# Delta rule of a two-block transformer kernel: from six units of full 128x128 blocks to three groups of compact 64x64 blocks, with the scan's steps placed between the levels of the next group's inverse

## What is computed

```python
diff = gc[..., :, None] - gc[..., None, :]            # gc: cumulated gates inside the chunk
decay = jnp.where(lower, jnp.exp(jnp.where(lower, diff, 0.0)), 0.0)
a_mat = jnp.where(strict, jnp.einsum('nbhid,nbhjd->nbhij', kb, kc) * decay, 0.0)
t_inv = lax.linalg.triangular_solve(eye + a_mat, eye, ...)   # inverse of a 64x64 unit triangle
u_val = t_inv @ vb
w_key = t_inv @ (kb * exp(gc))
attn_intra = jnp.where(lower, (qc @ kc.T) * decay, 0.0)
def step(s, xs):                                     # one chunk after the other
    v_new = u_i - w_i @ s
    o_i = qd_i @ s + a_i @ v_new
    s = s * jnp.exp(gl_i) + kd_i.T @ v_new
```

## Time and profile before

| | us |
|---|---|
| median of 3 runs (3429.64 to 3438.17) | 3431.32 |
| the profiled execution's own time | 3429.59 |
| its span | 3427.8 |
| PE busy (share of the span) | 3205.1 (94%) |
| DVE busy | 1474.0 (43%) |
| POOL busy | 1566.4 (46%) |
| ACT busy | 739.4 (22%) |
| DMA, mean over the span | 139 GB/s |

### The profile page before, as it was taken

The page is one execution under the profiler, slowest core; times in us unless marked ns, Lnnn a source line. Parts: engine busy times, 40 slices in busy tenths (PEclk is TensorE's granted clock), DMA queues, the critical chain, the costliest instruction groups (busy, mean ns, idle before and its releaser), DMA issues.

```text
span 3427.8 us, 39498 instructions
## 1 busy us (share of the span) xinstructions
PE 3205.1 (94%) x15738; PEld 2494.3 (73%) x15738; DVE 1474.0 (43%) x2741; ACT 739.4 (22%) x1544; POOL 1566.4 (46%) x1104
## 2 busy tenths in 40 slices
PE   6999999989999999999998999979998989879998
PEld 4767778767778776777877777766557888558876
DVE  2664433435550266444244555212204555267721
ACT  3333331111110233333111111001122111121110
POOL 5444555565546543445556455530003324156654
PEclk9999999999999999999999999979989999989999
DMA  5444444446666443444444666531100000135554
GB/s 185 145 133 138 152 149 165 149 151 229 229 226 196 160 148 123 148 142 144 163 154 147 210 243 229 178 136 44 61 25 1 1 1 1 37 112 191 195 181 144
DMA packets 129239, 477.03 MB, mean 139 GB/s; under 512 B 14352, under 2 KB 14352, under 8 KB 128160
## 3 DMA queue, kind: packets, MB, share of 16 engines
q1 hardware_dynamic: 70592, 261.23, 24.2%
q0 software_dynamic: 57024, 207.64, 16.8%
q10 hardware_dynamic: 1440, 5.64, 0.4%
HBM read 472.32 MB, written 2.13 MB: 138 GB/s over the span
## 4 chain that ended last, share of the span: by engine, by line
PE 79%; DVE 9%; issue 5%; POOL 4%; ACT 1%; DMA 1%; POOLq 0%; DVEq 0%; ACTq 0%
PE dense L673 18%; PE dense L675 17%; PE dense L674 17%; PE dense L756 7%; POOL raw_lo L2179 2%; PE scores L866 2%; PE O L900 1%; PE turned L1108 1%; PE scores L1117 1%; PE turned L888 1%; POOL squares_sum L2198 1%; PE scores L673 1%; PE scores L674 1%; PE scores L675 1%; PE O L934 1%
## 5 line engine op out<-in xcount | busy, mean ns | idle before, releaser
L2179 POOL TENSOR_TENSOR raw_lo<-raw,weights_hi 128x1024 fp32r<-128x1024 f32 x396 | 951.9, 2404 | 75.7 <-DMA raw<-stream 40.4
L673 PE MATMUL dense<-h_hi,weights_hi 128*128 128x512 f32 x2208 | 890.9, 403 | 31.8 <-POOL raw_lo L2179 16.3
L675 PE MATMUL dense<-h_hi,raw_lo 128*128 128x512 f32 x2208 | 867.6, 393 | 0.0
L674 PE MATMUL dense<-h_lo,weights_hi 128*128 128x512 f32 x2208 | 867.3, 393 | 0.0
L2172 POOL DMA_DIRECT2D weights_hi<-stream x396 | 228.9, 578 | 1090.4 <-PE dense L675 972.7
L673 PEld LDWEIGHTS dense<-h_hi,weights_hi 128*128 128x128 f32 x2208 | 419.4, 190 | 160.5 <-issue 68.1
L675 PEld LDWEIGHTS dense<-h_hi,raw_lo 128*128 128x128 f32 x2208 | 418.6, 190 | 91.2
L674 PEld LDWEIGHTS dense<-h_lo,weights_hi 128*128 128x128 f32 x2208 | 419.8, 190 | 80.9
L673 PE MATMUL dense<-hidden_hi,weights_hi 128*128 128x512 f32 x528 | 207.6, 393 | 10.9 <-POOL raw_lo L2179 6.3
L674 PE MATMUL dense<-hidden_lo,weights_hi 128*128 128x512 f32 x528 | 206.4, 391 | 0.0
L675 PE MATMUL dense<-hidden_hi,raw_lo 128*128 128x512 f32 x528 | 206.4, 391 | 0.0
(11 more groups left out here) (326 smaller groups left out, 4713.6 us busy)
## 6 DMA issues: line engine op xcount, KB each, us to landing
raw<-stream SPq DMA_DIRECT2D x473, 512.0 KB, 3.6
weights_hi<-stream POOLq DMA_DIRECT2D x396, 512.0 KB, 4.7
decays<-stream ACTq DMA_DIRECT2D x8, 512.0 KB, 4.3
gates<-f_scratch SPq DMA_DIRECT2D x2, 1536.0 KB, 9.7
x<-x_in SPq DMA_DIRECT2D x2, 1024.0 KB, 8.5
dft<-dft SPq DMA_DIRECT2D x4, 512.0 KB, 7.0
out<-x SPq DMA_DIRECT2D x4, 512.0 KB, 2.7
const<-consts SPq DMA_DIRECT2D x1, 1088.0 KB, 4.9
```

Source lines behind the costliest of these rows:

```text
L673: nc.tensor.matmul(banks[b], wh, xh, start=first, stop=False)
L674: nc.tensor.matmul(banks[b], wh, xl, start=False, stop=False)
L675: return nc.tensor.matmul(banks[b], wl, xh, start=False, stop=final)
L2179: nc.gpsimd.tensor_tensor(raw_lo(n % RAW_SLOTS), raw(n % RAW_SLOTS), w_hi(w % HI_SLOTS), ALU.subtract).then_inc(weights_lo, 1)
```

## The change

Every matrix of the stage is now compact: 128 x 512 holds 8 blocks of 64x64 per direction and partition half, that is two token blocks (j = 0, 1) times four heads side by side, and the two chunks of a token block one above the other (partitions 0 to 63 and 64 to 127). Two token blocks make a group; there are three groups of two blocks in place of six units.

- The decays of all three groups and both directions are made ahead of the k transposes: POOL multiplies the gates by a triangle (`rowsum`, 6 tiles), DVE makes `rowbar` (6 tiles), PE sums them by 12 products of 512 columns in the two dense banks, and ACT takes 6 exponentials.
- Key-key and query-key products are made once per group for both directions, as 64x64x64 products; A and X are then scaled by DVE with two instructions each, in place of 4 per head.
- Products of the inverse are 64x64x64 and use the tile corners (rows and columns 0 to 63, or 64 to 127, of the array) in turn. Only the update of TT is multiplied; T comes from TT by a DVE transpose (STREAM_TRANSPOSE) of 32x32 blocks, which is the whole transpose since up to level 4 all blocks are at most 32 wide. The update is written over Z in the same bank (`turned`).
- In place of scaled keys and values, POOL scales TT for w (`tt_gain`) and DVE scales TT for u (`tt_beta`).
- The four scan steps of group g - 1 stand between the levels 1 to 4 of group g: the read between Z and the update, the write behind the update. The last four steps stand alone. DVE decays the state ahead of the level's subtracts, and adds behind them; the output through the state is scaled by ACT, four instructions a direction (`output_state`).
- The third DMA of constants is smaller (1472 columns for 2176), and tiles of the stage lie at other places.

The new code of the stage, cut to its core (the removed functions `unit` and `scan` are shown above; the diff's DVE functions `make_a`, `make_x` and `level_zero`, ACT's part, the products for the outputs and the tables of places are left out; one `level_z` and one `level_update` of PE do both directions):

```diff
-UNITS = 6
+UNITS, GROUPS, STEPS = 6, 3, 12
 FIRST_L = 2
+PAIR_GDN = tuple([o[2 * g] // 2 for g in range(GROUPS)] for o in ORDER_GDN)
+LATENT_PAIRS = [(d, PAIR_GDN[d][g]) for g in (1, 2) for d in range(2)]
...
+                    nc.tensor.matmul(dense[:, k % 2, :], chunk_ones, rowsum[k], start=True, stop=False)
+                    nc.tensor.matmul(dense[:, k % 2, :], ident, rowbar[k], start=False, stop=True
+                                     ).then_inc(row_ready, 1)
...
+            def level_z(g, lev):
+                for d in range(2):
+                    pe.wait_ge(t_masked, level_no(g, lev, d))
+                    pe.wait_ge(t_ready_g, level_no(g, lev - 1, d))
+                    if lev == 1 and g:
+                        pe.wait_ge(u_copied, 4 * g)
...
+                                last = nc.tensor.matmul(turned[hs, d, c64(j, h)], a_level[d][hs, c64(j, h)],
+                                                        tt_mat[d][hs, c64(j, h)], start=True, stop=True)
+                    last.then_inc(t_z, 1)
+            def level_update(g, lev):
+                for d in range(2):
+                    pe.wait_ge(t_zc, turn_no(g, lev, d))
+                    for j in range(2):
                         for h in range(GH):
+                            for c in range(2):
+                                hs = half_rows(c)
+                                last = nc.tensor.matmul(turned[hs, d, c64(j, h)], t_mat[d][hs, c64(j, h)],
+                                                        z_mat[d][hs, c64(j, h)], start=True, stop=True)
+                    last.then_inc(t_upd, 1)
...
+                                last = nc.tensor.matmul((turned, scores)[c][:, d, c64(j, h)],
+                                                        ktok[half_rows(c), 2 * p + j, h * P:(h + 1) * P],
+                                                        tt_gain[d][half_rows(c), c64(j, h)], start=True, stop=True)
+                    last.then_inc(w_ready, 1)
...
+                        if j:
+                            pe.wait_ge(w_copied, 2 * g + d + 1)
                         for h in range(GH):
+                            for c in range(2):
+                                hs = half_rows(c)
+                                last = nc.tensor.matmul((dense, turned)[j][hs, d, h * P:(h + 1) * P],
+                                                        tt_beta[d][hs, c64(j, h)],
+                                                        vtok[hs, 2 * p + j, h * P:(h + 1) * P], start=True, stop=True)
+                        last.then_inc(u_ready, 1)
+            def scan_read(s):
+                n, i = s // 2, s % 2
+                pe.wait_ge(w_copied, 2 * (n // 2) + 2)
+                pe.wait_ge(u_copied, 4 * (n // 2) + 4)
+                if s:
+                    pe.wait_ge(c_s, 2 * s)
+                else:
+                    pe.wait_ge(ab_step, 14)
+                if latent_no(s) > 0:
+                    pe.wait_ge(c_o2, 2 * latent_no(s))
+                for h in range(GH):
+                    hc = slice(h * P, (h + 1) * P)
+                    for d in range(2):
+                        c, hs = chunk_of(d, i)
+                        last = nc.tensor.matmul(dense[hs, d, hc], wT[2 * d + c][:, c64(ORDER_GDN[d][n] % 2, h)],
+                                                state[d][:, hc], start=True, stop=True)
+                last.then_inc(c_ws, 1)
...
+            def scan_write(s):
+                n, i = s // 2, s % 2
+                pe.wait_ge(c_v, 2 * s + 2)
+                if s < STEPS - 1:
+                    pe.wait_ge(kd_ready, 2 * n + 2)
+                    for h in range(GH):
+                        hc = slice(h * P, (h + 1) * P)
+                        for d in range(2):
+                            c, hs = chunk_of(d, i)
+                            u = u_rows[2 * d + ORDER_GDN[d][n] % 2]
+                            last = nc.tensor.matmul((O[:], misc[:])[d][:, hc], kd[2 * d + n % 2][hs, hc], u[hs, hc],
+                                                    start=True, stop=True)
+                    last.then_inc(c_sd, 1)
...
+            for g in range(GROUPS):
+                for lev in range(1, LEVELS):
+                    level_z(g, lev)
+                    if g and lev < LEVELS - 1:
+                        scan_read(4 * (g - 1) + lev - 1)
+                    level_update(g, lev)
+                    if g and lev < LEVELS - 1:
+                        scan_write(4 * (g - 1) + lev - 1)
+                    if g == 0 and lev >= LEVELS - 2:
+                        turn_x(2 * (lev - LEVELS + 2))
+                        turn_x(2 * (lev - LEVELS + 2) + 1)
+                w_and_u(g)
+            for s in range(STEPS - 4, STEPS):
+                scan_read(s)
+                scan_write(s)
...
+            def level_done(g, lev):
+                for d in range(2):
+                    dve.wait_ge(t_upd, turn_no(g, lev, d))
+                    nc.vector.tensor_tensor(tt_mat[d], tt_mat[d], turned[:, d, :], ALU.subtract).then_inc(t_subbed, 1)
+                    if lev < LEVELS - 1:
+                        dve.wait_ge(t_subbed, level_no(g, lev, d))
+                        nc.vector.transpose(t_mat[d], tt_mat[d]).then_inc(t_ready_g, 1)
...
+            def new_values(s):
+                n, i = s // 2, s % 2
+                dve.wait_ge(c_ws, s + 1)
+                for d in range(2):
+                    c, hs = chunk_of(d, i)
+                    u = u_rows[2 * d + ORDER_GDN[d][n] % 2]
+                    nc.vector.tensor_tensor(u[hs, :], u[hs, :], dense[hs, d, :], ALU.subtract).then_inc(c_v, 1)
+                if s == STEPS - 1:
+                    return
+                if latent_no(s) >= 0:
+                    dve.wait_ge(c_qs, latent_no(s) + 1)
+                for d in range(2):
+                    c, hs = chunk_of(d, i)
+                    at = (c * 2 * XB + d * XB + ORDER_GDN[d][n]) * GH
+                    nc.vector.tensor_tensor(heads(state[d]), heads(state[d]), per_head(etot[:, at:at + GH]), ALU.mult
+                                            ).then_inc(c_decayed, 1)
+            def new_state(s):
+                n, i = s // 2, s % 2
+                if s < STEPS - 1:
+                    dve.wait_ge(c_sd, s + 1)
+                    for d in range(2):
+                        dve.wait_ge(c_decayed, 2 * s + d + 1)
+                        nc.vector.tensor_tensor(state[d], state[d], (O[:], misc[:])[d], ALU.add).then_inc(c_s, 1)
+                if latent_no(s) >= 0:
+                    dve.wait_ge(c_oi, latent_no(s) + 1)
+                    for d in range(2):
+                        c, hs = chunk_of(d, i)
+                        dve.wait_ge(c_o1, 2 * latent_no(s) + d + 1)
+                        dst = o2[ORDER_GDN[d][n]] if n < 4 else oscan[d]
+                        nc.vector.tensor_tensor(dst[hs, :], oscan[d][hs, :], dense[hs, d, :], ALU.add
+                                                ).then_inc(c_o2, 1)
+            dve.wait_ge(decay_done, 2 * GROUPS)
+            make_a(0)
+            for g in range(GROUPS):
+                level_zero(g)
+                for lev in range(1, LEVELS):
+                    if g and lev < LEVELS - 1:
+                        new_values(4 * (g - 1) + lev - 1)
+                    level_done(g, lev)
+                    if g and lev < LEVELS - 1:
+                        new_state(4 * (g - 1) + lev - 1)
+                    if g == 0 and lev < 3:
+                        make_a(lev)
+                    if g == 0 and lev in (3, 4):
+                        make_x(2 * lev - 6)
+                w_and_u(g)
+            for s in range(STEPS - 4, STEPS):
+                new_values(s)
+                new_state(s)
...
+            def mask(g, lev):
+                for d in range(2):
+                    if lev > 1:
+                        pool.wait_ge(t_z, turn_no(g, lev - 1, d))
+                    elif lev:
+                        pool.wait_ge(t_subbed, level_no(g, 0, d))
+                    else:
+                        pool.wait_ge(a_ready, 2 * g + d + 1)
+                        if g:
+                            pool.wait_ge(t_z, turn_no(g - 1, LEVELS - 1, d))
+                    nc.gpsimd.tensor_tensor(by8(a_level[d]), by8(a_mat[mat_no(d, PAIR_GDN[d][g])]), level_mask(d, lev),
+                                            ALU.mult).then_inc(t_masked, 1)
...
+            pool.wait_ge(row_ready, 2 * GROUPS)
+            for g in range(GROUPS):
+                for lev in range(LEVELS):
+                    mask(g, lev)
+                gained(g)
+                decayed_keys(2 * g)
+                decayed_keys(2 * g + 1)
+            for s in range(STEPS - 4, STEPS):
+                add_output(s)
```

More of the change, by code:

```diff
@@ L1491, in _ @@
                 nc.scalar.activation(vtok[:, t, :], bankB[t % 2], ACT.Copy).then_inc(v_stored, 1)
+            for k in range(2 * GROUPS):
+                act.wait_ge(row_ready, k + 1)
```

(16 more changed lines are left out.)

452 lines of the change are left out of this document (211 added, 241 removed).

## The result

The changed kernel takes 3266.06 us (median of 4 runs, 3265.16 to 3269.84); the kernel before takes 3430.48 in the runs beside it. The ratio is 0.9525, with a 95% interval of 0.9511 to 0.9538. Forecast was 3284, range 3252 to 3335: the sign and the range held, and the time is 18 us under the forecast.

The account below looks back on a forecast made before the run. PE was taken to bound the old levels, multiplying half-zero matrices. Span 3427.8 - 178 (walk) + 12 (meetings) + 10 (clock) + 9 (handoffs) = 3280.8; with 1.8 and 1.7 from span to median, forecast 3284, range 3252 to 3335.

Parts of the forecast that it names:

- Corners: Z and update products alternating between two opposite array corners: both run together, 0.030 us a record.
- corners in series: Rival: the corners do not run together, as both write one PSUM bank; 32 us more, 3316; chance 0.12.
- Head: Stage start, decays to first level's second Z: 12 sum products take 10.3 us, Z begins at 2602.2; 8 us dearer.
- Levels: Inverse levels of groups 0, 1 and 2: 5.4, 7.8 and 9.0 us each, bound by DVE.
- the walk: Stage's new order added up at trace prices, before extra costs: ends at 2760 instead of 2937.9, 178 us shorter.
- PE's busy time in the levels exceeds DVE's: Sign that the prediction is wrong; it expected DVE to bound the levels, with PE 5.6 busy of 7.8 us.
- (1) Meetings: DVE decays and scalings meeting POOL in SBUF: half of 0.8 us on each of 30 instructions, 12 us added.
- (2) Clock: Half-rate clock in the head, two turns and a little in the last steps: 10 us added.
- the turns: Stretches from one group's last level to the next's second Z, or to u copied: 18.2, 16.4 and 12.6 us.
- (3) Handoffs: Waits between engines through the stage: 5% of the 188 us from 2572 to 2760, 9 us added.
- Slower than before, in series in time: Rival: each corner product waits until the one before leaves the array, 0.275 us a record; 3750; chance 0.03.
- Half clock through the stage: Rival: the clock stays at 1.2 GHz through the stage since PE is less busy; 3359; chance 0.06.

Follow-up runs that it names:

- experiment 1: Changed kernel with each level's Z and update products issued all on the upper corner, then all on the lower, instead of alternating: median 3326.72 us, ratio 0.9692.
- experiment 5: Changed kernel with POOL's masks in group 0, from level 2 on, working on 64 of 512 columns: 3265.33 us, then median 3264.55, ratio 0.9526.
- b1: Changed kernel with the state decays of the eight woven steps moved from DVE to ACT: median 3260.65 us, ratio 0.9501.
- experiment 2: The kernel of experiment 1, unchanged, profiled twice more: 3316.42 and 3287.52 us.
- b2: Changed kernel with the next group's first two masks, identity minus mask and its transposes placed before w and u: median 3257.47 us, ratio 0.9499.
- b3: Changed kernel with the last four steps writing their output term into the turned tile's bank: median 3262.20 us, ratio 0.9504.
- e3: Changed kernel with the state decays of the eight woven steps left out: 3260.27 us, one run.
- e4: The kernel of experiment 5, group 0's masks from level 2 on 64 of 512 columns, profiled twice: 3265.33 us, then median 3264.55.
- b4: Changed kernel with the three edits of b1, b2 and b3 together: median 3245.95 us, ratio 0.9461.
- e2: Changed kernel with no scan step in a level; each group's four steps stand alone behind its w and u: 3293.74 us, ratio 0.9598.

## Why the prediction was right, and where its 18 us went

**Corners: right.** 0.029 a record for the 0.030 taken. The order decides it: the rival (corners in series) is experiment 1, with its stage at +22 where I had priced 28 to 32. Its price was right for groups 1 and 2 (+0.9 and +1.4 a level for +0.9 and +1.3) and too high for group 0 (+0.4 for +1.7): PE's two blocks of 3.2 us make a level of 6.5 and not 7.1, and the level that they replace was 6.1 and not 5.4. The floor of issue that I had thought possible at 0.0375 isn't there; that figure was a mean over the 2x2 transposes, which stand in pairs 0.01 to 0.02 apart. The Trainium skill, "TensorEngine Tiling (Array Packing)", section "Gotcha 1: PSUM Pressure", says that different row tiles can't access one bank at a time. That does not hold for these records: the corners (0,0) and (64,64) write one bank, on different partitions, at 0.029 each.

**Head: right.** The 12 products took the 10.3 us of the forecast. In the chain of waits the second Z begins at 2606.16, 2603.1 in the prediction's time, forecast 2602.2. The 0.9 us hold a meeting that I had not charged: the first of DVE's two identity minus mask takes 1.76 for 0.68, under POOL's second mask.

```profile
2601.41 1.76 DVE t_mat L2189
...
2606.16 1.15 PE turned L1149 x32
...
2645.68 3.57 PE turned L1149 x64
```

**Levels: right in size in groups 1 and 2, on DVE as said.** 6.11, 7.8 and 9.14 for 5.4, 7.8 and 9.0. (Without the meeting group 0 is at 5.16, experiment 5, so there the walk was 0.24 too long and the meeting came on top.) The transpose took 0.71 for 0.65. "PE's busy time in the levels exceeds DVE's", my condition for being wrong, holds by a little in groups 1 and 2 (25.13 for 24.72, 26.88 for 25.21). It misled nothing: PE's 25 us include blocks that overlap DVE's, and b1, which takes the decays from DVE alone, shortens a level of group 1 by nearly all of their 1.28, and one of group 2 by 0.6.

**What failed is the sum of costs put on the walk: 12 + 10 + 9 = 31 charged, 11.2 found** (the last add on POOL ends at 2771.2 in the prediction's time; the bare walk gave 2760.0).

- (1) Meetings, 12 charged, 2.1 found in the levels of group 0. The mechanism was right, the count and the size of one wrong. There three pairs of scalings met the masks, 0.95 us a pair for the narrow masks' 1.38, 1.08 for the plain time. The six tt_beta met POOL's scalings too (a pair takes 2.28), but u, which alone reads them, stands behind w on PE and waited for none (the first pair is ready at 2635.47, the first u begins at 2638.85). The 16 decays met nothing, for POOL's masks of a level are over before DVE comes to them (changed kernel, POOL and then DVE):

```profile
2655.89 2.59 POOL L2469 TENSOR_TENSOR a_level<-gdn_a,const 128x512 f32<-128x512 f32 x2 [5.27 <-PE turned L1149]
```

```profile
2659.61 1.28 DVE L2231 TENSOR_TENSOR state<-state,const 128x512 f32<-128x512 f32 x2
```

  The masks wait only for the Z before them, so they end at 2658.48, 1.1 us before the decays begin; I could have laid that out from the order, and assumed half of each of 30 instead. The Trainium skill, "SBUF — State Buffer", section "Who interferes with whom", has the second to come fully blocked until the first ends; by that a scaling under a mask would cost up to 1.3 us more. The trace agrees: 1.08 for the one that began 0.43 us behind the mask's start (experiment 5). The half of 0.8 that I charged to each of 30 is no cost that any of them had: an instruction pays for what is left of the POOL instruction when it comes, and nothing where it comes first.
- (2) Clock, 10 charged, 6.1 found of the 6.6 by which the turns are longer: 19.9, 18.1 and 15.8 for 18.2, 16.4 and 12.6. In turns 0 and 1 the first Z behind the gap runs at half rate: 3.57 us for 64 records in the chain above, and 3.35 (2.03 elsewhere). In turn 2 it is w and u, for 7 us, and costs 3.2 (11.41 for 8.17). Each of turns 0 and 1 also holds 0.4 us of a mask that waited for DVE (1.65 for 1.27). So two of my three places were right. In the head, the third, the clock stayed at 1.00 (first row of the windows), and the largest loss stands in the last turn, where I had charged none; that the clock also falls without a long gap I had not expected.
- (3) Handoffs, 9 charged, 2.5 found in what is left: 0.9 in the head, which is the meeting above, 0.2 and 0.6 in the levels of groups 1 and 2, 0.9 in the steps. The 5% came from the old level, where 5.38 and 0.57 make 5.95 of 6.17, which is 3.6% and not 5; and the walk already held the waits that they were to stand for. I take this term to have been counted twice.

These 11.2 instead of 31 would have made the forecast 3264.

**Slower than before, in series in time: wrong,** as its rows said. **Half clock through the stage:** not in the changed kernel; experiment 2 shows that it exists. There it lasts 84 us and costs 34, on a kernel whose levels have no gap on PE. What it would cost the changed kernel, which I had put at 85 us for the whole stage, no run shows.

## What to carry to other kernels

Half-filled matrices are worth splitting into compact blocks even at a small N, if successive products go to opposite corners of the array; the order of the loop alone is worth 22 us here, and 61 by the medians, since the clock comes on top. Once the matrix engine is relieved, the next saving is on the engine that bounds the new level (b1) and in the turns between groups (b2), not in what only the old bound needed. Before charging a contention, lay the two engines' instructions side by side in time: here 16 of the 30 assumed meetings could not happen, and six more were waited for by no one.

## What the runs showed of the hardware that I had not expected

- The granted clock falls while PE is busy, too. In the changed kernel, w of the last group has 1 us of idle time ahead and runs at half:

```profile
2735.00:2738.00 3.00, 2.27 (x38) 2.27 (x40) 2.68 (x3) 0.22 (x1) 3.00 (x3) 0.96 0.00 0
2738.00:2741.00 3.00, 3.00 (x32) 2.88 (x30) 0.00 (x0) 0.87 (x2) 3.00 (x4) 0.50 0.00 0
2741.00:2744.00 3.00, 3.00 (x31) 3.00 (x31) 0.69 (x1) 1.09 (x2) 0.56 (x1) 0.50 0.02 5
```

  In b2 the same w, with the same 0.98 us ahead, runs at 1.00. What tells them apart stays open. In the profiles this stretch, w and u, takes 11.4 us for 8.17 in the last turn of the changed kernel, of b1, b3 and e3, in the first turn of both e4, and nowhere in b2, b4 and e2. So an edit elsewhere can move or remove 3.2 us, and a difference of that size needs a look at the clock before it is put down to the edit.
- One kernel can have two times. With PE nearly without gaps the clock stayed at 0.50 for 84 us in one execution, and came back after 7 us in another, 29 us apart in time (3316.42 and 3287.52).
- What a saving leaves can depend on where the clock falls, in the same way each time: 2.85 us in the levels of group 0 left 0.8 and 0.9 us of the stage, in two profiles, with the slow w and u in the first turn and not in the last.
- DVE instructions with both inputs in SBUF and POOL's masks and scalings take turns as wholes. A DVE instruction that begins under a POOL one ends 0.54 to 0.56 us after that one's end, whatever the length of the POOL one: 2613.30 after 2612.76, 2612.38 after 2611.84 (narrow mask), 2634.03 after 2633.47 (`tt_beta` under `tt_gain`). POOL's masks that begin under a DVE one take 1.65 to 1.72 for 1.27.
